# Splitting the direct term of a blocked state-space read-out by time step, with the input kept in its natural order

## The reference

```python
proj = h @ w_in[l] + b_in[l]                       # 512 tokens x 4096
ua, za, ub, zb, ga, gb = jnp.split(proj, SPLITS, axis=-1)
# s5 branch on ua (512 channels = 32 groups of 16; 64 complex states a group)
_, _, s_re, s_im = lax.associative_scan(..., (a_re, a_im, bu_re, bu_im), axis=1)
y = einsum('blgp,gcp->blgc', s_re, c_re) - einsum('blgp,gcp->blgc', s_im, c_im)
y = y.reshape(bsz, seq, SSM_WIDTH) + d_skip * u
y = jax.nn.gelu(y)
ya = y * jax.nn.sigmoid(y @ w_glu + b_glu) * jax.nn.silu(za)
```

## Time and profile before

| | |
|---|---|
| time, median of 3 runs | 1705.53 us (1705.19 to 1708.62) |
| profiled execution, its own time | 1708.62 us |
| its span, first to last instruction | 1706.8 us |
| granted clock of TensorE, mean | 0.996 of full speed |
| PE busy | 1686.2 us, 99% |
| PEld busy | 1402.0 us, 82% |
| DVE, POOL, ACT busy | 1038.0, 1019.2, 560.6 us |

### The profile page before, as it was taken

The page is one execution under the profiler, slowest core; times in us unless marked ns, Lnnn a source line. Parts: engine busy times, 40 slices in busy tenths (PEclk is TensorE's granted clock), DMA queues, the critical chain, the costliest instruction groups (busy, mean ns, idle before and its releaser), DMA issues.

```text
span 1706.8 us, 24447 instructions
## 1 busy us (share of the span) xinstructions
PE 1686.2 (99%) x9142; PEld 1402.0 (82%) x9142; DVE 1038.0 (61%) x1514; ACT 560.6 (33%) x1019; POOL 1019.2 (60%) x675
## 2 busy tenths in 40 slices
PE   9999999999999999999999999999999999999998
PEld 7778888788888887789888888888888898887887
DVE  3457767677777863445477637756548548846173
ACT  3557777624233232203223125232222221113111
POOL 3437676565666764555666175666667645557663
PEclk8999999999999999999999999999999999999999
DMA  9213233132259862343432133334443344222332
GB/s 357 78 56 108 100 105 103 35 111 76 94 201 314 289 224 92 125 147 120 165 99 87 37 100 100 118 122 153 143 134 121 126 161 150 86 74 93 99 99 87
DMA packets 56760, 217.20 MB, mean 127 GB/s; under 512 B 6305, under 2 KB 8609, under 8 KB 53346
## 3 DMA queue, kind: packets, MB, share of 16 engines
q1 hardware_dynamic: 51634, 201.80, 35.0%
q10 hardware_dynamic: 5040, 14.22, 2.2%
HBM read 201.84 MB, written 14.16 MB: 127 GB/s over the span
## 4 chain that ended last, share of the span: by engine, by line
PE 92%; DVE 4%; ACT 1%; POOL 1%; DMA 1%; issue 0%; SPq 0%; DVEq 0%; POOLq 0%; ACTq 0%
PE PS L2036 27%; PE PS L2037 26%; PE PS L2038 26%; PE PS L2367 2%; PE PS L2383 2%; PE PS L786 2%; PE PS L573 1%; PE PS L2190 1%; PE PS L1434 1%; DMA X<-in_x 0%; DVE WA L1634 0%; PE PS L1440 0%; POOL WL L1954 0%; POOL PR L1979 0%; PE PS L2105 0%
## 5 line engine op out<-in xcount | busy, mean ns | idle before, releaser
L1954 POOL TENSOR_TENSOR WL<-RAW,WH 128x1024 fp32r<-128x1024 f32 (+3 forms) x233 | 601.1, 2580 | 19.5
L2036 PE MATMUL PS<-HH,WH 128*128 128x512 f32 (+1 forms) x1400 | 529.5, 378 | 2.8 <-POOL WL L1954 1.1
L2038 PE MATMUL PS<-HH,WL 128*128 128x512 f32 (+1 forms) x1400 | 524.7, 375 | 0.0
L2037 PE MATMUL PS<-HL,WH 128*128 128x512 f32 (+1 forms) x1400 | 524.5, 375 | 0.0
L1951 POOL TENSOR_SCALAR WH<-RAW 128x1024 fp32r<-128x1024 f32 (+3 forms) x233 | 258.1, 1108 | 295.6 <-PE PS L2038 280.4
L2036 PEld LDWEIGHTS PS<-HH,WH 128*128 128x128 f32 x1400 | 263.6, 188 | 57.5 <-issue 10.1
L2038 PEld LDWEIGHTS PS<-HH,WL 128*128 128x128 f32 x1400 | 263.5, 188 | 47.7
L2037 PEld LDWEIGHTS PS<-HL,WH 128*128 128x128 f32 x1400 | 263.6, 188 | 45.8
L1950 POOL TENSOR_TENSOR SC<-ONES 1x1 f32<-1x1 f32 x134 | 32.1, 239 | 281.8 <-PE PS L2038 281.8
L1979 POOL TENSOR_SCALAR PR<-PR,SC 128x768 f32<-128x768 f32 x47 | 109.5, 2337 | 69.8 <-DVE SC L3080 69.8
L2036 PE MATMUL PS<-HIDH,WH 128*128 128x512 f32 (+1 forms) x396 | 148.4, 375 | 0.0
(11 more groups left out here) (435 smaller groups left out, 2778.8 us busy)
## 6 DMA issues: line engine op xcount, KB each, us to landing
RAW<-in_wup SPq DMA_DIRECT2D x88, 512.0 KB, 3.5
MRF<-in_modw SPq DMA_DIRECT2D x52, 512.0 KB, 4.6
RAW<-in_wdn SPq DMA_DIRECT2D x32, 704.0 KB, 4.1
MR<-in_modw SPq DMA_DIRECT2D x28, 512.0 KB, 3.5
RAW<-in_whin SPq DMA_DIRECT2D x28, 512.0 KB, 3.5
MK<-in_modk SPq DMA_DIRECT2D x8, 1024.0 KB, 9.9
RAW<-in_whead SPq DMA_DIRECT2D x8, 640.0 KB, 4.9
RAW<-in_wo SPq DMA_DIRECT2D x8, 512.0 KB, 3.5
```

Source lines behind the costliest of these rows:

```text
L1954: pool.tensor_tensor(WL[s][:, 0:n], raw[:, 0:n], WH[s][:, 0:n].bitcast(F32), ALU.subtract).then_inc(tile_split, 1)
L2036: pe.matmul(out, wh, xh, start=first, stop=False)
L2037: pe.matmul(out, wh, xl, start=False, stop=False)
L2038: return pe.matmul(out, wl, xh, start=False, stop=last)
```

## The change

The input is stored in its natural token order: ACT's fill becomes a plain copy with bias, and `ua_t` becomes a view with a step of four words. So `drive` reads its 128 moving columns with a step of 16 bytes. In `read_out` the direct term's matmuls go inside the loop over places: for place t and group i, t + 1 matmuls of 128 columns, whose moving operand also has the step of 16 bytes, and right behind them the eight matmuls of the states' contribution to the same 128 output columns.

```diff
-            ua_t = UA[:, :, :].rearrange("p a (t k) -> p a t k", t=T5)
+            ua_t = UA[:, :, :].rearrange("p a (k t) -> p a t k", t=T5)
...
-                for i2 in range(2):
-                    i = 2 * hh + i2
-                    for q in range(T5):
-                        pe.matmul(PS[:, 6 + i2, NC5 * q:L], KB2[:, i, q, :], UA[:, i, 0:L - NC5 * q], start=q == 0, stop=False)
                 for t in range(T5):
                     for i2 in range(2):
                         i = 2 * hh + i2
+                        out = PS[:, 6 + i2, NC5 * t:NC5 * t + NC5]
+                        for q in range(t + 1):
+                            pe.matmul(out, KB2[:, i, q, :], ua_t[:, i, t - q, :], start=q == 0, stop=False)
                         for part, s in enumerate((SRE, SIM)):
                             for mm in range(4):
-                                m = pe.matmul(PS[32 * mm:32 * mm + 32, 6 + i2, NC5 * t:NC5 * t + NC5],
-                                              CB2[:, part, t, 4 * i + mm, :], s[:, mm, i2, :], start=False, stop=part == 1 and t == T5 - 1)
+                                m = pe.matmul(out[32 * mm:32 * mm + 32, :], CB2[:, part, t, 4 * i + mm, :],
+                                              s[:, mm, i2, :], start=False, stop=part == 1)
                 m.then_inc(S["cmm"], 1)
...
-                    ins = act.activation(UA[:, f, :].rearrange("p (t k) -> p t k", t=T5),
-                                         src.rearrange("p (k t) -> p t k", t=T5), ACT.Identity, bias=par("bin2", f), scale=1.0)
+                    ins = act.activation(UA[:, f, :], src, ACT.Identity, bias=par("bin2", f), scale=1.0)
```

## The result

The changed kernel takes 1727.44 us (median of 4 runs, 1727.26 to 1728.67); the kernel before had 1706.09 beside it. The ratio is 1.0124, 95% interval 1.0111 to 1.0136: 21.2 us slower (the two medians are 21.35 apart). The direction was forecast, the size was not: +5.6 was predicted, and 1727.4 lies just outside the range that ended at 1727.0. All 24 executions of it on record lie between 1726.01 and 1728.86 us, so the end of the range falls inside the scatter; the point forecast is 16 us off.

The account below looks back on a forecast made before the run. PE, busy 99% of the span, was taken to bound the kernel. Shape changes 4.8, columns 0.2 and stepped reading 0.6 made +5.6 us on the median of 1705.53, so 1711.1 us; range 1707 to 1727.

Parts of the forecast that it names:

- ACT's fill costs nothing: Filling the input on ACT: stepped 687 ns, plain 688, neither on the path, so no change.
- Columns +0.2 us: Direct term of both read-outs: same columns in more, 128-column instructions, +0.2 us, bounds 0.0 and 0.3.
- Shape changes +4.8 us: Read-outs: 14 more pairs of switches between whole-array and 32-column matmuls, in and out, 0.34 us each, +4.8 us.
- Reading with a step +0.6 us: Drives and read-outs: 144 passes of 128 columns reading 16 bytes apart, 0.004 us each, +0.6 us; ends 0 and 18.7.
- One-to-one on the path, 0.35 swallowed: PE's gains or losses show fully, except in its 0.35 us wait before read_out(0).
- rival 1: Drives and read-outs: the stepped read halves the pace, 0.108 us more a pass, 1725.7 us in all; chance 0.22.

Follow-up runs that it names:

- e3: Kernel before, place-major input, direct term cut into 128-column matmuls, all ahead of the states' part: 1707.22 against 1707.53 us, ratio 1.000.
- e1: Kernel before, place-major input, direct term cut into 128-column matmuls and mixed with the states' part: 1711.88 against 1707.53 us, ratio 1.003.
- e7: Kernel before, place-major input, direct term cut and mixed, each matmul split into four of 32 output columns: 1708.43 against 1706.93 us, ratio 1.001.
- e2: Kernel before with natural-order input, moving reads stepped by 16 bytes, direct term still wide: 1723.53 against 1707.53 us, ratio 1.0093.
- e4: Kernel before, drive(0) reading with a step of two words, drive(1) of three, output not the reference's: one execution, 1708.56 us.
- e8: Kernel before, glu tiles reading shifted, in pairs or pairs four apart, drives in pairs straddling 16-byte lines; output not the reference's: one execution, 1715.06 us.
- e6: Kernel before, four glu tiles reading their 512 moving columns with steps of one to four words, output not the reference's: one execution, 1714.92 us.

## Why the prediction was wrong

Point by point, in its own steps:

- *ACT's fill costs nothing*: right, 687 ns in both.
- *Columns +0.2 us*: right. e3 gives +0.15 a read-out in the trace, 0.3 for both, which is the upper bound, and no measurable time.
- *Shape changes +4.8 us*: right in mechanism and size. e1's read-out is 10.59 us, as worked out from the earlier trace rows, and e1 as a whole is +4.35 us; e7's read-outs show that the shape is the cause. In the changed kernel itself a pair leaves 0.31 instead of 0.34, so 4.3 to 4.8.
- *Reading with a step +0.6 us*: wrong, and this is the step that failed. It measured 16.0 us alone (e2). In the changed kernel's trace: 2 × 14.98 − 8.11 − 8.04 = 13.8 us more in the read-outs, of which 4.3 are shape changes and 9.5 are 80 passes at 0.226 instead of 0.108; the drives are 7.44 and 7.45 instead of 3.79 and 3.78, 7.3 more; less the swallowed 0.35. The sum is 20.8, measured 21.2. (The 4.3 is what a pair leaves once the passes are taken at 0.226; e1 and e2 measure the two parts apart, +4.35 and +16.0, together 20.4.)
- *One-to-one on the path, 0.35 swallowed*: right. The wait is gone, the others stand as before.

How did the step go wrong? The bounds were 0 and 18.7, from a reading that is stretched 2.2 times, and the truth, 16.5, lay in them. For the point I took "the row nearest in kind", L573 and L758. But those are weight loads and not moving operands, and they read with a step of two words, which leaves two words on each line; the change reads with four, one word a line. e4 shows that this is just where the cost begins: 3.96 us at two, 5.77 at three (e4), 7.52 at four (e2). L573's 0.004 told the price of the free side of that edge. The argument that a float32 pass asks only half of `linear`'s rate "so there is room" was wrong too: fp32r with gaps gives a column in 0.9 ns, plain float32 with one word a line needs 1.76 to 1.8. So one reading rate does not describe both kinds.

L758's reading, stretched 2.2 times, which spoke for rival 1, came nearer to what plain float32 shows, by its size and not by its step: in these runs two words a line cost a moving operand 3% (3.96 us a drive against 3.85), one costs a factor of 2.0 to 2.1 (waves 0.227 and 0.233 us apart against 0.112). For fp32r the count of lines does not tell the pace: two neighbours on a line every eight words run at half speed all the same (e8, 0.461 us against 0.227), and more lines cost no more (e6, 0.450 at step three against 0.451 at step two). I gave rival 1 a chance of 0.22 and should have made it the forecast. The second slip is in the range: rival 1 was priced at exactly twice, 0.108 us more a pass and 1725.7 us. No row and no run shows exactly twice; the changed kernel shows 0.226 a pass, 0.118 more. And the range was cut to 1727.0 although my own upper row, 0.24 a pass, led to 1728 and more. With the measured 0.226 the result falls at that edge.

## What to carry to other kernels

For plain float32, price a pass by the 16-byte lines its moving operand touches (waves of 128 columns: 0.114 us for 64 lines, 0.227 for 128), and don't let a row with one pattern stand for another across that edge: a layout turned while ACT copies a PSUM bank out was free here (687 against 688 ns), while reading it turned on the matrix engine cost 16 of 1706 us. Don't alternate whole-array matmuls with 32-column ones in a stream; group them (e3), and 0.3 us a pair is saved (e1 is 4.35 us slower with 14 pairs more). Writing both in the same shape (e7) saves it inside the read-out too, but that kernel had more instructions and lost 1.85 us to a stop. Where bounds are far apart and the nearest row differs in just the thing that changes, keep the far bound whole in the range.

## What the runs showed that was not expected

- Matmuls of 32 output columns were mixed with others of the same shape without loss in their pace: e7's 160 direct instructions of a read-out, in waves of four, kept the 0.11 us wave. The one stop of 1.57 us, in the second read-out, is the open end of that run.
